# One order of experts turned around, and half a weight slot released in mid product

## What is computed

```python
def _hier_moe(x, w_group, b_group, w_expert, b_expert, w_up, w_down):
    ...
    g_sel = jnp.argmax(g_logits, axis=-1)
    ...
    top_w, top_i = lax.top_k(e_prob, TOP_K)
    ...
    expert_id = g_sel[:, None] * EXPERTS_PER_GROUP + top_i
    ...
    for e in range(N_EXPERTS):
        a, b = jnp.split(t @ w_up[e], 2, axis=-1)
        y = y + combine[:, e:e + 1] * ((jax.nn.silu(a) * b) @ w_down[e])
    return y.reshape(B, L, D)
```

## Time and profile before

| | |
|---|---|
| median of 3 runs | 1102.53 us |
| lowest and highest | 1102.08, 1105.09 us |
| profiled execution: own time | 1102.75 us |
| its span | 1100.9 us |
| TensorE busy | 1023.8 us, 93% of the span |
| VectorE, ScalarE, GpSimd busy | 596.7, 207.9, 316.7 us |
| moved by DMA | 319.00 MB, mean 290 GB/s |
| mean granted TensorE clock | 0.969 |

### The profile page before, as it was taken

One profiled execution on the slowest core, in us unless ns is written; L12 is line 12 of the kernel. 1 busy time (PEld: TensorE's weight loads), 2 busy tenths in 40 slices (PEclk: granted clock), 3 DMA queues, 4 the chain that ended last, 5 costly groups with the idle time before them and its releaser, 6 DMA issues.

```text
span 1100.9 us, 25728 instructions
## 1 busy us (share of the span) xinstructions
PE 1023.8 (93%) x10516; PEld 613.6 (56%) x10516; DVE 596.7 (54%) x1392; ACT 207.9 (19%) x497; POOL 316.7 (29%) x425
## 2 busy tenths in 40 slices
PE   8999999899989999999969999999988999999773
PEld 2545555385556666666545554575465666666441
DVE  6447998745553333333489991575574333333226
ACT  3143223001410000000140000462231100000002
POOL 1200000410135555555310000254014555555332
PEclk9999999999999999999989999699989999999997
DMA  9954478940699999999976786433087996999991
GB/s 336 402 226 146 177 247 296 397 178 1 237 406 403 406 405 406 354 406 405 369 283 246 267 324 267 134 97 87 0 328 284 377 406 264 403 386 405 405 364 57
DMA packets 101832, 319.00 MB, mean 290 GB/s; under 512 B 8417, under 2 KB 12705, under 8 KB 101377
## 3 DMA queue, kind: packets, MB, share of 16 engines
q1 hardware_dynamic: 91858, 299.65, 70.8%
q0 software_dynamic: 5776, 17.30, 4.6%
q10 hardware_dynamic: 4128, 1.05, 0.4%
HBM read 312.22 MB, written 5.77 MB: 289 GB/s over the span
## 4 chain that ended last, share of the span: by engine, by line
PE 74%; DVE 8%; DMA 6%; SPq 5%; issue 2%; ACT 2%; POOL 2%; DVEq 0%; ACTq 0%; POOLq 0%
PE bank L759 72%; SPq L492 5%; DMA ring<-in_moe_w_down 4%; PE bank L1195 1%; POOL P L733 1%; DVE st L1943 1%; DMA group_row<-token_rows,rows_now 1%; DVE P L2001 1%; DVE hT L1721 1%; DMA row_beta<-in_ln_b 1%; ACT x L1356 1%; PE bank L957 0%; DVE x L1747 0%; SPq L502 0%; DVE x L2046 0%
## 5 line engine op out<-in xcount | busy, mean ns | idle before, releaser
L759 PE MATMUL bank<-ring,xgT 128*32 128x256 f32 x4224 | 243.0, 381 | 7.5 <-DMA ring<-in_moe_w_up 5.1
L759 PE MATMUL bank<-hT,ring 128*128 128x384 f32 x640 | 209.0, 489 | 2.8 <-DVE hT L1721 2.7
L759 PEld LDWEIGHTS bank<-ring,xgT 128*32 128x32 f32 x4224 | 144.8, 110 | 87.6 <-issue 8.7
L1908 DVE TENSOR_TENSOR he<-sa,bank 128x128 f32<-128x128 f32 x66 | 19.0, 288 | 297.7 <-ACT sa L1402 297.7
L759 PEld LDWEIGHTS bank<-hT,ring 128*128 128x128 f32 x640 | 122.2, 191 | 89.1 <-issue 6.0
L1544 DVE CUSTOM_DVE_ANT_0 ring<-ring,ring 128x1024 f32<-128x1024 f32 x120 | 146.8, 1224 | 4.6 <-PE bank L759 1.0
L759 PE MATMUL bank<-ring,heT 128*32 128x256 f32 x2112 | 129.1, 385 | 8.7 <-DMA ring<-in_moe_w_down 8.7
L759 PE MATMUL bank<-yg,ohT 32*128 32x256 f32 x1632 | 107.3, 391 | 3.2 <-DVE yg L1937 2.9
L759 PEld LDWEIGHTS bank<-ring,heT 128*32 128x32 f32 x2112 | 63.2, 110 | 64.8 <-issue 32.0
L713 POOL TENSOR_TENSOR yg<-ysb,gate_s 128x256 f32<-128x256 f32 x128 | 91.0, 733 | 18.8 <-ACT ysb L1407 11.2
L759 PEld LDWEIGHTS bank<-yg,ohT 32*128 32x128 f32 x1632 | 74.6, 184 | 36.0 <-issue 26.3
(11 more groups left out here) (278 smaller groups left out, 1118.9 us busy)
## 6 DMA issues: line engine op xcount, KB each, us to landing
ring<-in_moe_w_up SPq DMA_DIRECT2D x64, 2048.0 KB, 21.8
ring<-in_moe_w_down SPq DMA_DIRECT2D x32, 2048.0 KB, 18.5
ring<-in_k_ada SPq DMA_DIRECT2D x15, 2048.0 KB, 9.6
ring<-in_w_ada SPq DMA_DIRECT2D x9, 2048.0 KB, 13.0
ring<-in_na_w_qkv SPq DMA_DIRECT2D x6, 2048.0 KB, 13.3
ring<-in_hy_w_in SPq DMA_DIRECT2D x5, 2048.0 KB, 13.1
ring<-in_hy_w_out SPq DMA_DIRECT2D x2, 2048.0 KB, 11.9
ring<-in_na_w_out SPq DMA_DIRECT2D x2, 2048.0 KB, 10.7
```

The costliest lines, as they stand in the source:

```text
L759: return nc.tensor.matmul(out, lhsT, rhs, start=first, stop=last)
L1908: v.tensor_tensor(he[:], sa[:], ps[0][:, 128:256], ALU.mult).then_inc(S["he_ready"], 1)
```

## The change

Two parts. In the order: an added VectorE operation (`turn_sign`) gives -2 where the first four experts have more than 8 groups together, and 0 elsewhere; a second one makes `order_key` key x sign + key, the negative key or the key itself. In the ring: the last matmul with the first up half increments a new semaphore `up_half`, and SyncE waits for that one, instead of `up_ready`, before it loads over a first up half.

```diff
+FIRST_USUAL = 2 * FIRST
...
+        turn_sign = at("turn_sign", [128, 1], RM + 3776)
...
                         groups = sp.value_load(NBi[0:1, NB_CUM + 1 + e:NB_CUM + 2 + e], min_val=1, max_val=MAX_BLOCKS)
-                        sp.wait_ge(S["up_ready"], groups)
+                        sp.wait_ge(S[("up_half", "up_ready")[c]], groups)
...
                             for q in range(4):
                                 last = mm(ps[0][32 * q:32 * q + 32, 0:256].rearrange("s (g n) -> s g n", n=32),
                                           xgT[:, k, :], w[:, q, :, :], k == 0, k == KT - 1)
+                            if k == 3:
+                                last.then_inc(S["up_half"], 1)
                         last.then_inc(S["up_ready"], 1)
...
                 link(v.scalar_tensor_tensor(out=order_key[:], in0=blocks, scalar=float(EXPERTS), in1=iota, op0=ALU.mult, op1=ALU.subtract))
+                link(v.tensor_scalar(turn_sign[:], nbase[:, EXPERTS + FIRST:EXPERTS + FIRST + 1], FIRST_USUAL + 0.5, -2.0, ALU.is_gt, ALU.mult))
+                link(v.scalar_tensor_tensor(out=order_key[:], in0=order_key[:], scalar=turn_sign[:], in1=order_key[:],
+                                            op0=ALU.mult, op1=ALU.add))
```

More of the change, by code:

```diff
@@ L395, in build @@
             moe_sems.append({n: sem(f"{n}{l}") for n in (
-                "oh_pair", "oh_ready", "gathered", "picks_ready", "list_summed", "list_ready", "hot_ready", "picks_step", "rows_named", "rows_stored", "x_added", "rows0_in", "rows1_in", "xgT_ready", "up_ready", "sa_ready",
+                "oh_pair", "oh_ready", "gathered", "picks_ready", "list_summed", "list_ready", "hot_ready", "picks_step", "rows_named", "rows_stored", "x_added", "rows0_in", "rows1_in", "xgT_ready", "up_half", "up_ready", "sa_ready",
                 "he_ready", "heT_ready", "y_ready", "ysb_ready", "yg_ready", "ohk_ready", "ohT_ready", "srow_ready", "combined")})
```

## The result

The changed kernel takes 1092.32 us (median of 4 runs, 1091.70 to 1094.17) beside 1103.10 us before; the ratio is 0.9907, 95% interval 0.9887 to 0.9927. The forecast was 1090.6 us, a ratio of 0.989. The profiled execution took 1092.32 us itself, span 1090.5: 10.4 us less than the profiled one of before.

A forecast was written before the change was run, and what follows sets the result against it. Layer 1 was taken as bound by late expert weights (13.3 us of TensorE waits), layer 0 by TensorE. Layer 1 gains 12.6 us, layer 0 loses 0.7: 1102.5 - 11.9 = 1090.6 us, range 1086 to 1096.5.

The forecast's parts named there:

- The hole: Layer 1, 918 to 931 us: weight stream stands still (DMA share 0.33) with all ring slots taken; the turned order removes it.
- piece 11: Layer 1 weight load of 2 MB, forecast issued at 851.9 us; its line put the last landing at 1056.1.
- piece 26: Layer 1 weight load freed by group 15, forecast issued at 934.5 us; its line put the last landing at 1058.0.
- piece 32: Layer 1 weight load freed by group 20, forecast issued at 969.0 us; its line put the last landing at 1060.2.
- The two weight waits: Layer 1, TensorE at the last two down pieces: 3.9 us in all instead of 13.3, 1.7 of it at the first.
- the middle of two lines: Layer 1's last landing taken as 1059.1 us, midway between the lines of piece 26 (1058.0) and piece 32 (1060.2).
- Halves: Weight ring: first up half released after 32 of the up product's 64 records, 1.7 us earlier.
- the third line of the prediction: Layer 1, the line of piece 32: 969.0 + 16 x 5.38 + 5.1 = 1060.2 us, an upper end for the last landing.
- Increments: TensorE up products: one semaphore increment inside each costs 0 to 0.08 us, taken as 0.02; 0.7 us in layer 0.
- Added operations: Two small VectorE operations before the positions and first gather: 0.4 us a layer, on the chain, range 0 to 0.5.
- the clock behind the last wait: Layer 1's last down product: full speed (1.93 us) after a wait near 2 us, so 8.6 us from landing to end.
- The rival of TensorE as the bound: Layer 1: the weight stream catches up, no wait is left, last product ends at 1063.8, time 1086.6 us; chance 0.10.

The follow-up runs named there:

- order_only: Changed kernel with the early release of the first up half undone, the turned order kept: 1092.38 us, ratio to before 0.9912.
- half_only: Changed kernel with the threshold set so high that the order never turns, early release and added operations kept: 1101.64 us, ratio 0.9991.
- ticks: Changed kernel plus six more semaphore increments, which nobody waits for, in every up product: 1092.56 us, ratio 0.9908.
- sign_only: Changed kernel with the order never turned and the early release undone, leaving only the two added VectorE operations: 1103.98 us, ratio 1.0011.
- filled: Changed kernel plus 14 unread TensorE products before the first group's down-piece wait in layer 1's last two experts: 1092.35 us, ratio 0.9912.
- one_last: Changed kernel with layer 1's last one-group expert moved to the very end by four more VectorE operations: 1087.43 us, ratio 0.9866.
- always_turned: Changed kernel with the threshold set to 0, so the order turns in layer 0 too: 1100.59 us, ratio 0.9984.

## Why the prediction was right, and where it was off

**The hole was the cause.** The stations of the stream came nearly as worked out: piece 11 at 852.43 (forecast 851.9), piece 26 at 934.82 (934.5), piece 32 at 969.14 (969.0), piece 29 at 941.72 (near 941), the last landing at 1059.58 (1059.1). The two weight waits that were left are 1.45 and 2.12 us (1.7 and 2.2). The landing is so near in part by luck: the middle of two lines was a choice, and each line by itself was off, with 123.5 us from piece 26 on where it took 124.8, and 91.2 us from piece 32 on where it took 90.4. order_only shows that the order alone brings the gain, half_only that without it the time doesn't move.

**Halves.** The release comes 1.7 us earlier, as forecast (half_only); counted from the layer's second product the last landing of order_only is 1.4 to 1.7 us later, where the third line of the prediction would have given 1.7. But no time of an execution follows that can be told from none: 0.9912 with the order alone, 0.9907 with both. The prediction gave the halves no sum of their own, and a reader might take the 1.7 us in its lines for part of the gain. That they were worth it isn't shown. The forecast hardly depended on them: without them its own terms give a landing at 1060.4 instead of 1059.1 and nothing for increments, which is 1091.2 us instead of 1090.6. The gain that it gave the halves and the price that it put on their increments nearly cancel, so the close number speaks for neither.

**Increments.** 0.02 us each was too much, and so was the 26 ns that the prediction set beside it; ticks puts them near 0. Layer 0, forecast at +0.7 us, took 0.2 less from start to end than before (227.48 against 227.69 without its wait). Its first product began 0.55 us later, forecast 0.4, and the weight wait of 0.4 disappeared, as forecast.

**Added operations.** 0.46 us a layer measured, 0.4 taken. The gather of layer 1 didn't hide them up to the first product (sign_only).

**The step that was mis-sized is the clock behind the last wait.** The prediction let waits of about 2 us pass without a slow product, from the one row of 2.12 us. In the profiled execution such a wait was followed by a product of 3.60 us instead of 1.93: 1.7 us, and with the landing 0.5 us late and 0.7 us saved in layer 0 that is the 1.5 us between the forecast gain of 11.9 and the 10.4 us of the profiled execution. It isn't a constant cost of the change: order_only had its slow product where a later wait took it up, filled had none and took just as long. What decides whether such a product is slow stays open.

**The rival of TensorE as the bound** (1086.6 us) was not reached because the last down piece is late for a two-group expert. one_last, which asks for it one group later, gets to 1087.4 us without a weight wait, four more VectorE operations included: the rival's arithmetic holds for an order that ends well.

## What to carry to other kernels

This rests on two layers of one kernel. Where weights stream through a ring and are used for times that vary, look at how the slot releases lie in time, not only at the sums: one long user while all slots are full stops the stream, and the time comes back as waits at the very end. Put short users ahead of the first long one if the stream has a lead, and the long one first if it has none (the turned order won 10 us in layer 1 and lost 9 in layer 0). And let the last user be the one with the least work behind its last piece.

## What the runs showed of the hardware

A product behind a wait ran at the lower level of the clock (1.2 GHz, granted clock about 0.5) or at the full one (2.4 GHz, 1.00), and the length of the wait alone did not decide. For instance waits of 2.14 us in order_only and 2.12 us in the changed kernel were followed by 3.56 and 3.60 us, while 2.12 us before was followed by 1.93 us; always_turned had a wait of 3.47 us and then a product of 3.38, while half_only had waits of 3.60 and 3.41 us and behind each a product of 1.93.

The gather for the second product of layer 1 runs while the weight stream keeps the DMA engines busy (share 1.01 from 834 to 843 us before). From its issue to its landing it took 7.35 us before, 7.97 in the changed kernel and 9.07 in one_last, and TensorE waited 0.93 us for it in the changed kernel, not at all in order_only, 2.04 us in one_last. With the slow product that can follow, this may be a part of the spread between executions of one kernel; only one execution of each was traced, so that isn't shown.

The stream under load differed as well: from the issue of piece 32 to the last landing it took 1059.58 - 969.14 = 90.4 us in the changed kernel and 1059.16 - 968.62 = 90.5 in order_only, but 1061.64 - 969.53 = 92.1 in filled. Why is not known.
